# The split activations hs, moved from beside the weight buffers to the far end of SBUF

## What is computed

```python
def swiglu(h, w_gate, w_up, w_down):
    return (jax.nn.silu(h @ w_gate) * (h @ w_up)) @ w_down
...
        h = rms_norm(x, attn_norm[l])
        proj = h @ w_in[l]
...
        x = x + mixed @ w_out[l]
        h = rms_norm(x, ffn_norm[l])
        x = x + (jax.nn.silu(h @ w_ffn_gate[l]) * (h @ w_ffn_up[l])) @ w_ffn_down[l]
    return rms_norm(x, final_norm)
...
        x = x + 0.5 * swiglu(rms_norm_2(x, ffn1_norm[i]), ffn1_w_gate[i], ffn1_w_up[i], ffn1_w_down[i])
        h = rms_norm_2(x, mix_norm[i])
        fq, fk, fv, f_logit, sq, sk, sv, g_fox, g_sb = split_columns(h @ w_in[i])
...
        x = x + jax.nn.sigmoid(rms_norm_2(x, ple_norm[i]) @ w_ple_gate[i]) * (p[i] @ w_ple_proj[i])
```

## The kernel before

| buffer | before | after |
|---|---|---|
| x | 16,512 | 16,512 |
| hs | 24,704 to 41,088 | 212,672 to 229,056 |
| raw | 41,088 | 24,704 |
| whi (slot 1 is 8,320 further) | 57,728 to 74,368 | 41,344 to 57,984 |
| wlo | 74,368 to 91,008 | 57,984 to 74,624 |
| con (constants) | 95,104 to 109,472 | 78,720 to 93,088 |
| arena begins | 112,960 | 96,576 |
| hid | 112,960 to 158,016 | 112,960 to 158,016 |
| osplit of the first block, ms1 | from 137,536 | from 121,152 |
| ms2 | 112,960 | 184,640 |
| d_p (probabilities of the first attention) | 125,248 | 108,864 |
| he (factors of the recurrence) | from 212,352 | from 195,968 |

## Time and profile before

### The profile page before, as it was taken

One profiled execution on the slowest core, in us unless ns is written; L12 is line 12 of the kernel. 1 busy time (PEld: TensorE's weight loads), 2 busy tenths in 40 slices (PEclk: granted clock), 3 DMA queues, 4 the chain that ended last, 5 costly groups with the idle time before them and its releaser, 6 DMA issues.

```text
span 1180.2 us, 22335 instructions
## 1 busy us (share of the span) xinstructions
PE 1117.5 (95%) x8828; PEld 1075.6 (91%) x8828; DVE 738.5 (63%) x1079; ACT 627.3 (53%) x963; POOL 54.7 (5%) x64
## 2 busy tenths in 40 slices
PE   3999898998999999999999997999898999999998
PEld 3899797988999999999999996887778999999998
DVE  3788797635776655567555666444545776555566
ACT  4446755467465444465444344455757564444453
POOL 0000000000420000120000010000000220000010
PEclk9999999999999999999999998998989999999999
DMA  6344433234455554565455453343212455554563
GB/s 211 100 149 163 151 128 119 101 107 148 175 185 207 178 179 145 198 225 180 178 183 176 160 196 142 143 142 108 105 41 108 178 204 187 182 186 158 192 216 108
DMA packets 31997, 187.14 MB, mean 159 GB/s; under 512 B 4032, under 2 KB 7488, under 8 KB 14144
## 3 DMA queue, kind: packets, MB, share of 16 engines
q1 hardware_dynamic: 31936, 186.28, 44.9%
HBM read 184.43 MB, written 1.05 MB: 157 GB/s over the span
## 4 chain that ended last, share of the span: by engine, by line
PE 81%; DVE 8%; ACT 5%; issue 3%; DMA 1%; POOL 1%; SPq 0%; DVEq 0%; POOLq 0%; ACTq 0%
PE acc L587 73%; PE area_a L587 4%; PE area_t L587 3%; DVE wlo L1411 2%; ACT whi L1051 1%; ACT L1051 1%; ACT he L1051 1%; POOL mixed L1972 1%; DMA raw<-in_w_projT_a 1%; PE area_t L826 1%; ACT gates L1051 0%; DMA raw<-in_w_fvl 0%; DVE s_after L1936 0%; DVE score L1633 0%; DVE st L1585 0%
## 5 line engine op out<-in xcount | busy, mean ns | idle before, releaser
L587 PE MATMUL acc<-hs,whi 128*128 128x256 f32 x3584 | 658.3, 286 | 16.9 <-DVEq L1420 7.8
L587 PEld LDWEIGHTS acc<-hs,whi 128*128 128x128 f32 x3584 | 564.1, 193 | 24.9 <-DVEq L1420 12.0
L587 PE MATMUL acc<-hs,wlo 128*128 128x256 f32 x1792 | 510.6, 285 | 0.0
L1051 ACT ACTIVATE whi<-raw 128x1024 fp32r<-128x1024 f32 (+2 forms) x378 | 357.4, 980 | 162.1 <-PE acc L587 143.6
L1411 DVE TENSOR_TENSOR wlo<-raw,whi 128x1024 fp32r<-128x1024 f32 (+3 forms) x258 | 271.4, 1094 | 158.4 <-ACT whi L1051 157.8
L587 PEld LDWEIGHTS acc<-hs,wlo 128*128 128x128 f32 x1792 | 345.7, 193 | 0.0
L587 PE MATMUL acc<-hid,whi 128*128 128x256 f32 x1056 | 180.0, 276 | 0.3 <-DVE wlo L1411 0.3
L587 PEld LDWEIGHTS acc<-hid,whi 128*128 128x128 f32 x1056 | 159.0, 188 | 0.5 <-DVE wlo L1411 0.5
L587 PE MATMUL acc<-hid,wlo 128*128 128x256 f32 x528 | 145.8, 276 | 0.0
L1490 DVE TENSOR_TENSOR wlo<-raw,whi 128x1024 fp32r<-128x1024 f32 x120 | 141.1, 1217 | 3.5 <-ACT whi L1051 3.5
L1503 DVE TENSOR_TENSOR hbuf<-acc,sbuf 128x256 f32<-128x256 f32 x66 | 28.0, 424 | 133.6 <-PE acc L587 130.1
(11 more groups left out here) (308 smaller groups left out, 1061.3 us busy)
## 6 DMA issues: line engine op xcount, KB each, us to landing
raw<-in_w_gu SPq DMA_DIRECT2D x66, 1024.0 KB, 4.8
raw<-in_w_dn SPq DMA_DIRECT2D x48, 704.0 KB, 4.0
raw<-in_w_up SPq DMA_DIRECT2D x10, 1024.0 KB, 4.8
raw<-in_w_gates1b SPq DMA_DIRECT2D x8, 1024.0 KB, 4.9
raw<-in_w_out SPq DMA_DIRECT2D x8, 1024.0 KB, 4.8
raw<-in_w_qk SPq DMA_DIRECT2D x8, 1024.0 KB, 4.9
raw<-in_w_gates SPq DMA_DIRECT2D x8, 1024.0 KB, 4.8
raw<-in_w_projT_b SPq DMA_DIRECT2D x7, 1024.0 KB, 4.8
```

The source lines that it names most:

```text
L587: return nc.tensor.matmul(out, w, m, start=start, stop=stop, skip_group_check=True)
L1051: return nc.scalar.activation(out, in_, f, **kw)
```

## The change

`hs` is no longer placed between `x` and `raw`, but behind the arena, at `base + 4 * ARENA`, and with it `sq`, the squares of the first norm, which share its bytes. All that came behind `hs` moves 16,384 bytes down, the arena too, whose length is now the constant ARENA. Inside the arena `hid` starts 4,096 elements later, which leaves it on the bytes it had; its small companions gbuf, sbuf and hbuf take the place in front of it; `ms2` goes from offset 0 to 22,016. No instruction is added, taken away or moved on any engine, and no wait changes: only addresses do.

```diff
+ARENA = 29024
...
         x = fixed("x", (KD, T))
-        hs_off = top[0]
-        hs = fixed("hs", (KD, 2 * T), F32R)
         raw = fixed("raw", (2, SLOT))
         whi = fixed("whi", (2, SLOT), F32R)
         wlo = fixed("wlo", (2, SLOT), F32R)
...
-        sq = at("sq", (KD, T), hs_off)
         xr = fixed("xr", (T,))
         ones_row = fixed("ones_row", (T,))
         base = top[0]
+        hs_off = base + 4 * ARENA
+        assert hs_off + 4 * KD * 2 * T <= nc.sbuf_usable_end
+        hs = at("hs", (KD, 2 * T), hs_off, F32R)
+        sq = at("sq", (KD, T), hs_off)
 
         def arena(name, off, shape, dt=F32):
-            assert base + 4 * (off + int(np.prod(shape))) <= nc.sbuf_usable_end, name
+            assert off + int(np.prod(shape)) <= ARENA, name
             return at(name, shape, base + 4 * off, dt)
...
         ms1 = arena("ms1", 6144, (KD, 2 * T), F32R)
-        ms2 = arena("ms2", 0, (KD, 2 * T), F32R)
-
-
-        hid = arena("hid", 0, (KF, 2 * T), F32R)
-        gbuf = arena("gbuf", 11264, (2, T))
-        sbuf = arena("sbuf", 12288, (2, T))
-        hbuf = arena("hbuf", 12800, (2, T))
+        ms2 = arena("ms2", 22016, (KD, 2 * T), F32R)
+
+
+        hid = arena("hid", 4096, (KF, 2 * T), F32R)
+        gbuf = arena("gbuf", 0, (2, T))
+        sbuf = arena("sbuf", 1024, (2, T))
+        hbuf = arena("hbuf", 1536, (2, T))
```

## The result

| | before | after |
|---|---|---|
| median, us | 1184.53 (4 executions, 1183.12 to 1187.39) | 1171.51 (4 executions, 1170.61 to 1173.39) |
| profiled execution, us | 1182.07 | 1173.39 |
| its mean PE clock | 0.977 | 0.965 |

The ratio is 0.989, with a 95% interval of 0.987 to 0.9911. The change is worth 13.0 us; 27.5 were forecast, and 1171.5 lies just inside the stated range.

A forecast was written before the change was run, and what follows sets the result against it. The PE was taken as the bound, through the start-to-start distance of matmuls from hs (119.2 ns, to become 113.4). Savings of 19.5 + 8 = 27.5 us took the median from 1185.55 to 1158.0 us; range 1151 to 1172.

The forecast's parts named there:

- no effect: Rival: the distance between matmuls belongs to something else that goes with hs; time 1185.5 us, chance 0.08.
- slower: Rival: distance between matmuls depends on how far apart the two streams start; 32 us more, 1217 us, chance 0.04.
- the low bits: Reading: hs is slow because it and the weights start at multiples of 128 bytes; hid, ms, osplit are 64 off.
- the border between 96 and 113 KB: Reading: memory has regions divided there, and two PE streams in one region disturb each other.
- (a): w_gu and w_pg, 3360 matmuls from hs on a PE-only chain: 5.8 ns less each, 19.5 us.
- (b): Mixers, 2016 matmuls from hs, chain shared with VectorE and ScalarE: 8 us saved, bounds 3 and 11.7 us.
- half-way rival: Matmuls from hs fall into the rhythm of 118 ns and stay: 6.5 us saved, 1179 us, chance 0.07.
- the share of 0.80: First mixers, 27 to 280 us: 119 of 149 us of matmuls from hs taken to be on the chain.
- the step from 10 to 8 us: Mixers: saving reduced because a shorter chain gives way to one through VectorE.
- the foreseen sign: Longer waits for VectorE between 27 and 280 us would show the mixers' saving overrated, if the whole gained under 20 us.
- (c): w_gu: splits and weight stream behind the PE keep up at 5.44 us a tile, costing nothing; cover 2.8 us per pair.
- The next bound: Rival: mixers give nothing back and w_gu waits for a transfer or split every other tile; 1171 us, chance 0.04.

The follow-up runs named there:

- near layout: Kernel before with hs moved 64 bytes, still beside the weights, all behind it 128 bytes: 1163.75 us, ratio 0.9822; repeated 1169.61 us, ratio 0.9851.
- near layouts: Kernel before with hs moved 64 bytes (1163.75 us), or with 64 unused bytes between hs and raw (1166.07 us); profiles include variants of these.
- the far ones: Layouts with fast hs at the far end, five profiles: the kernel after (1171.51 us), its repetition (1172.72), and its variants with filling or reordered w_fvl.
- the cut: Kernel before with one of 24 matmuls left out in 50 of the first mixer's 52 output blocks from hs: 1184.99 us against 1186.43, ratio 0.9991.
- the filled pair: Kernels before and after, each with 11 products of constants in the pause ahead of w_fvl: 1184.74 and 1163.69 us.
- the plain one: Kernels before and after without filling products: 1184.53 and 1171.51 us.
- hs32: Kernel before with hs moved 32 bytes and all behind it 128 bytes: 1174.97 us, ratio 0.9937.

## Why the prediction was right and wrong

**Right: what bounds the kernel, and that an address sets it.** No instruction moved, and PE's runs got shorter by the distance between starts alone. Of the rivals, no effect and slower are out. By the Trainium skill, "SBUF — State Buffer", section on who interferes with whom, PE never waits on anyone for SBUF; the three layouts with 120.2 us and the three with 114.5 to 114.9 us for the same 1008 matmuls show a cost of place, so for this kernel the measurement decides against the rule. It is not another engine that PE meets, as far as seen: the distance is 120 ns with VectorE and ScalarE idle.

**Settled: of the two readings, the low bits.** Nothing remains of the border between 96 and 113 KB. The title's far end is incidental; what helped is that 212,672 is 64 off a multiple of 128 and the weights' 41,344 is not. More closely it is the difference of the two. As foreseen, the slots no longer differ in the kernel after: 113.3 ns in both. The difference of the slots before, which the rival of the slower kernel put down to how far apart the streams start, goes with their places modulo 256.

**(a) Right in size: 19.5 forecast, 18.0 measured** (17.1 in the w_gu stages, 1.0 behind w_dn2). With hs near the weights the same stages give 19.7 (6.26 + 5.96 + 6.27 + 1.17). Both fast layouts have tiles in a second rhythm, many in the mixers and up to four in a w_gu stage, as these rows of the timeline of after show, first the fast one, then the other, both in the first mixers (start, duration):

```profile
97.10 0.39 PE L589 MATMUL acc<-hs,whi 128*128 128x256 f32 x2
...
97.78 0.39 PE L589 MATMUL acc<-hs,whi 128*128 128x256 f32 x2
...
152.85 0.40 PE L589 MATMUL acc<-hs,whi 128*128 128x256 f32 x2
...
153.91 0.28 PE L589 MATMUL acc<-hs,whi 128*128 128x256 f32 x1
```

0.68/6 = 113 ns, and 1.06/9 = 118 ns. In after the first three tiles of w_gu0 run at 117.8, in the near layout none: 3 x 48 x 4.5 ns = 0.65 us, all of what w_gu0 is longer there (120.71 against 120.10).

**(b) Wrong: 8 us forecast, some 2 to 3 measured.** Two parts of the step failed. First, its distance: the term took 5.8 ns for all 2016 matmuls of the mixers. It fell from 119.3 to 116.4 ns in the first ones and from 119.1 to 115.8 in the second, 6.2 us of PE work in place of 11.7. The half-way rival had seen the rhythm of 118 in a tile behind a stall; it gave it to all matmuls or to none, and it is true of tiles that make up more than half of them in the mixers ((116.4 - 113.3)/4.5 = 0.7 in the first, 0.6 in the second), where stalls are frequent, and of few in w_gu. Secondly, the share of 0.80. In part it was misread: the chain's line for acc holds all products into the accumulators, and with the chain split up by operand only 106 of its 119 us have hs moving, a share of 0.71, and 74 of the 86 us in the second mixers, 0.81. For the rest the chain gave way to VectorE more than the step from 10 to 8 us allowed for. With the half clock taken out, the near layouts are 1.7 us shorter for 4.4 us less PE work (1248 x 3.5 ns), the far ones 1.8 us for 3.4 (1248 x 2.7, mean of five), the cut 2.6 us for 6.0: by this estimate the share is 0.4 to 0.5, and the foreseen sign, more waiting for VectorE, is there in PE's idle time (17.7 to 19.2 us). That the near layouts gained 3.3 us in this stage and the far ones 1.0 is the clock's doing, 4.7 against 7.1 us. In the second mixers w_qk gives 0.8 to 1.4 us, and the rest varies from 161.8 to 168.0 us among profiles of either kind of layout, which hides what 384 matmuls could give.

**(c) Right.** Splits and stream kept up; DMA has 0.53 in w_gu. The next bound, which was given 1171 us, didn't appear: the time met its number for another reason.

**Wrong: "every term is a change of the distance".** The sum had no term for the clock and so put it at nothing without a reason, though the kernel before ran w_fvl's start at 0.50. It measured 8.9 us in the profiles, and 8 between the filled pair and the plain one (21.05 - 13.0). With the term the account closes: 18.0 from (a) and 2 to 3 from (b) make 20 to 21, beside 21.05 measured with the clock held; less 8 to 9 it is 11 to 13.

**Open.** Why the clock comes back later in the faster layouts was not found, nor why it stays up at two places of the first mixers in the near ones alone. It is not fixed by the layout: one execution of after in ten had 0.978 and 1160.5 us, the kernel with the cut has the old layout and 24.4 us of w_fvl, and hs32 has executions of both kinds. Shown is that the low stretch gets short when the narrow matmuls don't stand between the wide ones, that the clock then falls behind the narrow ones, and that the low stretch isn't there when the pause is filled. What selects the rhythm of 113.3 or 117.8 ns after a stall stays open as well.

## What to carry to other kernels

Where PE is the bound, divide an unbroken run of matmuls by their number for each moving operand; if two operands of one shape differ, try 64 bytes more between the moving operand and the weights before any reordering. A kernel that gets shorter can lose part of its gain to the clock in a stage that the change doesn't touch, so compare stages and their granted clock, not only the sum; the same goes for an experiment that measures what a stage gives back. A pause ahead of dense PE work can be filled with products of constants, as many as PE's idle time there is long: six of them were worth 11 us in after.

## What the hardware showed that was not expected

- Moving operand and weights at the same place modulo 128 bytes: 119.2 ns from start to start for a 128x128 by 128x256 product in fp32r; 64 bytes apart 113.6 ns (114.48/1008); 32 bytes apart 117.1. Of those at the same place modulo 128, the ones at the same place modulo 256 take 119.9 ns, the others 118.6.
- The same matmul at the same relative place has two steady rhythms, 113.3 and 117.8 ns; nearly every tile holds one of them.
- Dense PE work of 512-column matmuls with 8-column ones between them ran without a gap for up to 26 us at the 1.2 GHz level; with the wide ones in a row the full clock was back after 5.5 us. Behind twenty-four narrow ones in a row it fell from 1.00 to 0.50, 1.2 us after the last of them.
- A product of two float32 operands with 512 columns is recorded as two matmuls, 0.87 us in all (9.61/11).
